# A hybrid attention and conv-FFN step on one core: five edits around two stage borders and the placement of the feed-forward operands

## The reference

```python
h = rms_norm(x, norm_attn)
qa, ka, va, qb, kb, vb = project_heads(h, ...)       # one projection, QK-norm, rope on the b part
oa = band_attn_a(qa, ka, va, rel_table)              # own chunk of 64 and 8 before it, bias by distance
ob = window_attn_b(qb, kb, vb, sinks)                # own chunk and 2 before it, with sinks
x = x + concat(oa, ob) @ w_out
h2 = rms_norm(x, norm_ffn)
gate, up = split(h2 @ w_gate_up)                     # 2 x 2816 columns
y = silu(causal_conv3(gate)) * up
x = x + y @ w_down
```

## Time and profile before

| | |
|---|---|
| Median of 3 runs | 2585.76 us (2584.2 to 2586.54) |
| Profiled execution, its own time | 2588.3 us |
| Span of its instructions | 2586.5 us, mean granted clock 0.98 |
| PE busy | 2447.7 us, 95% |
| DVE, ACT, POOL busy | 67%, 45%, 39% |
| DMA | 577.88 MB, mean 223 GB/s |
| project, attend, combine, ffn begin near | 0, 476.8, 945, 1176.5 us |

### The profile page before, as it was taken

The page is one execution under the profiler, slowest core; times in us unless marked ns, Lnnn a source line. Parts: engine busy times, 40 slices in busy tenths (PEclk is TensorE's granted clock), DMA queues, the critical chain, the costliest instruction groups (busy, mean ns, idle before and its releaser), DMA issues. The chain is left out here.

```text
span 2586.5 us, 46395 instructions
## 1 busy us (share of the span) xinstructions
PE 2447.7 (95%) x15365; PEld 2338.7 (90%) x15365; DVE 1740.0 (67%) x3774; ACT 1165.4 (45%) x2658; POOL 1003.2 (39%) x1153
## 2 busy tenths in 40 slices
PE   6999999589999979997999999999999999999998
PEld 4888888489999979987899999989999998999997
DVE  7667565466767755777676666766666777666766
ACT  6232322377776753334444443543444454444433
POOL 2888888557788778841220000213000021000001
PEclk9999999789999989998999999999999999999999
DMA  8776766656666659878686666878766677666665
GB/s 257 218 225 207 222 209 193 149 143 178 177 164 182 184 168 350 299 278 310 218 295 214 210 209 214 302 235 301 221 210 216 214 265 263 209 212 213 218 202 182
DMA packets 318493, 577.88 MB, mean 223 GB/s; under 512 B 35490, under 2 KB 168082, under 8 KB 318178
## 3 DMA queue, kind: packets, MB, share of 16 engines
q1 hardware_dynamic: 274288, 423.85, 51.9%
q0 software_dynamic: 39728, 149.36, 18.1%
q10 hardware_dynamic: 4290, 2.31, 0.4%
HBM read 444.88 MB, written 132.10 MB: 223 GB/s over the span
## 5 line engine op out<-in xcount | busy, mean ns | idle before, releaser
L2170 PE MATMUL ffn_x<-carry_big 128*128 128x352 f32 x2508 | 461.9, 325 | 17.6 <-PEq L62 13.5
L2170 PEld LDWEIGHTS ffn_x<-carry_big 128*128 128x128 f32 x2508 | 414.4, 189 | 22.6 <-issue 20.4
L2170 PE MATMUL ffn_z<-ffn_h_hi_S,carry_big 128*128 128x352 f32 x1056 | 283.7, 330 | 17.3 <-DVE carry_big L2311 11.2
L316 PE MATMUL project_z<-project_w_hi,project_h_hi 128*128 128x512 f32 (+3 forms) x680 | 256.3, 377 | 20.1 <-DVE project_w_lo L489 16.0
L316 PE MATMUL project_z<-project_w_lo,project_h_hi 128*128 128x512 f32 (+3 forms) x680 | 252.5, 371 | 0.0
L316 PE MATMUL project_z<-project_w_hi,project_h_lo 128*128 128x512 f32 (+3 forms) x680 | 252.4, 371 | 0.0
L2071 POOL TENSOR_TENSOR carry_x<-carry_x,carry_work 128x352 f32<-128x352 f32 x48 | 52.2, 1088 | 514.2 <-DVE carry_work L2429 455.8
L2065 POOL DMA_DIRECT2D carry_work<-h_sums_scratch x8 | 4.4, 552 | 584.0 <-DVE ffn_y_lo_S L2333 579.6
L2311 DVE TENSOR_TENSOR carry_big<-carry_w_raw,carry_big 128x512 fp32r<-128x512 f32 (+2 forms) x413 | 225.2, 553 | 0.7 <-ACT carry_big L2250 0.4
L946 PE MATMUL attend_o<-attend_v,attend_prob_t 128*128 (+1 forms) x1680 | 213.1, 271 | 0.0
L946 PEld LDWEIGHTS attend_o<-attend_v,attend_prob_t 128*128 128x128 f32 x1680 | 211.0, 194 | 0.6
(11 more groups left out here) (259 smaller groups left out, 6534.5 us busy)
## 6 DMA issues: line engine op xcount, KB each, us to landing
carry_big<-t_gu_scratch SPq DMA_DIRECT2D x264, 512.0 KB, 4.0
carry_big<-t_dn_scratch SPq DMA_DIRECT2D x240, 256.0 KB, 3.3
carry_w_raw<-w_gu SPq DMA_DIRECT2D x198, 256.0 KB, 4.1
t_gu_scratch<-project_quads POOLq DMA_DIRECT2D x68, 512.0 KB, 4.5
carry_w_raw<-w_dn SPq DMA_DIRECT2D x180, 128.0 KB, 3.5
project_quads<-w_quads POOLq DMA_DIRECT2D x68, 256.0 KB, 4.6
carry_w_raw<-w_o SPq DMA_DIRECT2D x24, 512.0 KB, 6.0
t_dn_scratch<-attend_quads POOLq DMA_DIRECT2D x22, 512.0 KB, 4.4
```

Of the source, the lines that this page charges most:

```text
L316: last = nc.tensor.matmul(z[c][0:w, 0:width], h[:, k, 0:w], ww[:, k, first:first + width], start=(k == 0 and h is hi and ww is w_hi), stop ...
L2170: mm = nc.tensor.matmul(bank[:, 0:SUB], weights(c)[:, wp, k, :], (hi, lo)[a][name][:, 1 if short else k, :], start=first and k == 0 and (w ...
```

## The change

1. **attend.** The cache loads go to SP ahead of everything, and the first tile's queries go from SP to ACT behind bias, far and sink. The identity and the cached values go to POOL, ahead of its memsets. The caches' lo parts go from POOL to DVE, behind the bias and ahead of `split_first`.
2. **combine, sums.** S3, S1, S2 are made by DVE in step 2, s = 0, of the last block, S4 in step 3, s = 0. S3's split moves from step 3, s = 0, to step 2, s = 1. POOL keeps the two loads and the two stores. A12 gets a buffer of its own and is loaded by SP in step 2, behind the next weights and ahead of the stores of x1 and h2. S4 takes the buffer of A11.
3. **Last square.** The square of the last row tile moves from combine to ffn's c0 on ACT (`last_square`), and its addition to DVE at c0 (`last_add`). DVE adds the one before it inside the last step.
4. **Norm in ffn.** PE's sum moves from c0 to c5, ACT's root from c0 to c6, DVE's correction from c0 to c7 and the eight `last_norm` from c4..c11 to c8..c15. ACT's wait for A12's lo part at c3 is gone.
5. **Placement.** `gate` is allocated before the operands and not behind them.

```diff
# attend
@block.sync
-            load(0)
+            for (first, count, cache), src in zip(caches, (ka_cache..., kb_cache...)):
+                twice(cache, src, cache_ld)
+            twice(raw[:, HEADS:HEADS + KV_A, 0:DEC], k_a[:, :, SEQ:]..., ld)
+            twice(raw[:, HEADS + KV_A:, 0:DEC], qk_b[PAIRS_B:, :, SEQ:]..., ld)
+            sp.dma_start(v[0:DEC, TILES + 1, :], v_all[SEQ:, :]).then_inc(ld, 16)
             load_b(0)
@block.gpsimd
+            pool.dma_start(ident_sb[:], ident).then_inc(const_ld, 16)
+            pool.dma_start(v[:, TILES, 0:PAIRS_A * P], va_cache).then_inc(const_ld, 16)
+            pool.dma_start(v[:, TILES, PAIRS_A * P:], vb_cache).then_inc(const_ld, 16)
...
-            for i, (head, count, cache) in enumerate(caches):
-                part = keys[HEAD:, head:head + count, SEQ:SEQ + P]
-                pool.wait_ge(k0_hi, i + 1)
-                nc.gpsimd.tensor_tensor(part, cache[HEAD:, :, :], part.bitcast(F32), ALU.subtract).then_inc(k0_ok, 1)
@block.scalar
-            (cache loads, ident, va_cache, vb_cache)
+            for i in range(2):
+                nc.scalar.dma_start(raw[i * HEAD:(i + 1) * HEAD, 0:HEADS, 0:DEC], q_a[:, :, SEQ:]...).then_inc(ld, 16)
@block.vector
             dve.wait_ge(bias_set, 1)
+            for i, (head, count, cache) in enumerate(caches):
+                part = keys[HEAD:, head:head + count, SEQ:SEQ + P]
+                dve.wait_ge(k0_hi, i + 1)
+                nc.vector.tensor_tensor(part, cache[HEAD:, :, :], part.bitcast(F32), ALU.subtract).then_inc(k0_ok, 1)
             split_first()
# Carry
-        self.last_c = by_sub(part(0))
+        self.last_sq, self.last_t, self.last_r = part(1), by_sub(part(1)), by_sub(part(0))
-        self.first_raw = {"A12": self.stage[0], ...}
+        self.first_raw = {"A12": self.p_sum, ...}
# combine, SP
                     load_w(g + 1)
+                if (b, i) == (LAST, 2):
+                    sp.wait_ge(c_ok, LAST)
+                    stored(sp, range(HALF_K, KD))
+                    sp.dma_start(kept.first_raw["A12"], h2T[HALF_K:KD, :, 0:SUB]...).then_inc(kept.h0_ld["A12"], 16)
...
             pass_on(LAST, PAIRS - 1)
-            sp.wait_ge(kept.h_lo_ok, HALF_K)
-            sp.wait_ge(sums_ok, 3)
-            stored(sp, range(HALF_K, KD))
-            sp.dma_start(kept.first_raw["A12"], ...)
# combine, ACT
-                    square(b, 2 * i + s)
+                    if (b, i, s) != (LAST, PAIRS - 1, 1):
+                        square(b, 2 * i + s)
...
+                    if (b, i, s) == (LAST, 2, 1):
+                        split_first("S3")
                     if (b, i, s) == (LAST, PAIRS - 1, 0):
-                        split_first("S3")
                         split_first("S2")
# combine, DVE
+                    if (b, i, s) == (LAST, PAIRS - 1, 1):
+                        add_square(LAST, KD - 2)
                     add(b, i, s, 0)
...
+                    if (b, i, s) == (LAST, 2, 0):
+                        sum_s3()
+                        sums_s1_s2()
+                    if (b, i, s) == (LAST, 2, 1):
+                        split_first("S3")
                     if (b, i, s) == (LAST, PAIRS - 1, 0):
-                        split_first("S3")
+                        sum_s4()
                         split_first("S2")
...
-            for s in range(2):
-                add_square(LAST, KD - 2 + s)
# combine, POOL
-                (waits and the four tensor_tensor of L1671 to L1679)
                 pool.wait_ge(sums_ok, 2)
+                pool.dma_start(h_sums[0, 0], lower[1]).then_inc(sums_st[0], 16)
                 pool.wait_ge(sums_ok, 4)
+                pool.dma_start(h_sums[0, 3], kept.stage[0]).then_inc(sums_st[1], 16)
# ffn
+    LAST_NORM = 6
+        gate = m.sbuf("gate", [P, H + BLOCK])
         h_hi, h_lo = ...
         y_hi, y_lo = ...
-        gate = m.sbuf("gate", [P, H + BLOCK])
-            pool.wait_ge(last_c, 1)
+            pool.wait_ge(h_lo_ok, h_done(0, "A12", HK - 1))
             pool.dma_start(first_raw["S4"], h_sums[0, 3]).then_inc(h0_ld["S4"], 16)
-                if c == 0:                       # PE
+                if c == LAST_NORM - 1:
+                    pe.wait_ge(last_sum, 1)
                     (the sum of squares into kept.ms)
-                if c == 3:                       # ACT
-                    act.wait_ge(h_lo_ok, h_done(0, "A12", HK - 1))
-                if c == 0:
+                if c == LAST_NORM:
                     last_root()
                 if c == 0:                       # DVE
-                    last_scale()
+                    last_add()
+                if c == LAST_NORM + 1:
+                    last_scale()
-                if 4 <= c < 4 + KD:
-                    last_norm(c - 4)
+                if LAST_NORM + 1 < c <= LAST_NORM + 1 + KD:
+                    last_norm(c - LAST_NORM - 2)
```

More of the change, by code:

```diff
@@ L790, in store @@
                     .then_inc(o_st[mixer], 16)
-            load(0)
+            for (first, count, cache), src in zip(caches, (ka_cache.rearrange(by_heads, p=HEAD), kb_cache.rearrange("(a p) n -> p a n", p=HEAD))):
+                twice(cache, src, cache_ld)
+            twice(raw[:, HEADS:HEADS + KV_A, 0:DEC], k_a[:, :, SEQ:].rearrange(by_heads, p=HEAD), ld)
+            twice(raw[:, HEADS + KV_A:, 0:DEC], qk_b[PAIRS_B:, :, SEQ:].rearrange(by_heads, p=HEAD), ld)
+            sp.dma_start(v[0:DEC, TILES + 1, :], v_all[SEQ:, :]).then_inc(ld, 16)
             load_b(0)
@@ L1070, in _ @@
             nc.scalar.dma_start(sink[:], sinks.rearrange("(a n) -> a n", a=1)).then_inc(sink_ld, 16)
-            for (first, count, cache), src in zip(caches, (ka_cache.rearrange("f (a p) n -> p (f a) n", p=HEAD),
-                                                           kb_cache.rearrange("(a p) n -> p a n", p=HEAD))):
-                for i in range(2):
-                    nc.scalar.dma_start(cache[i * HEAD:(i + 1) * HEAD], src).then_inc(cache_ld, 16)
-            nc.scalar.dma_start(ident_sb[:], ident).then_inc(const_ld, 16)
-            nc.scalar.dma_start(v[:, TILES, 0:PAIRS_A * P], va_cache).then_inc(const_ld, 16)
-            nc.scalar.dma_start(v[:, TILES, PAIRS_A * P:], vb_cache).then_inc(const_ld, 16)
+            for i in range(2):
+                nc.scalar.dma_start(raw[i * HEAD:(i + 1) * HEAD, 0:HEADS, 0:DEC], q_a[:, :, SEQ:].rearrange("f (a p) n -> p (f a) n", p=HEAD)).then_inc(ld, 16)
             act.wait_ge(cache_ld, 64)
@@ L1252, in __init__ @@
         self.carry, self.tail, self.state = (self.small[:, i * 2 * KF:(i + 1) * 2 * KF].rearrange("p (f n) -> p f n", n=2) for i in range(3))
-        self.first_raw = {"A12": self.stage[0], "S1": self.s_all, "A22": self.y_raw, "S4": self.p_sum}
+        self.first_raw = {"A12": self.p_sum, "S1": self.s_all, "A22": self.y_raw, "S4": self.p_sum}
         flat = lambda first, count: self.big[:, first:first + count]
@@ L1402, in _ @@
                     load_w(g + 1)
+                if (b, i) == (LAST, 2):
+                    sp.wait_ge(c_ok, LAST)
+                    stored(sp, range(HALF_K, KD))
+                    sp.dma_start(kept.first_raw["A12"], h2T[HALF_K:KD, :, 0:SUB].rearrange("k p n -> p k n")).then_inc(kept.h0_ld["A12"], 16)
                 if b < LAST:
@@ L1421, in _ @@
             pass_on(LAST, PAIRS - 1)
-            sp.wait_ge(kept.h_lo_ok, HALF_K)
-            sp.wait_ge(sums_ok, 3)
-            stored(sp, range(HALF_K, KD))
-            sp.dma_start(kept.first_raw["A12"], h2T[HALF_K:KD, :, 0:SUB].rearrange("k p n -> p k n")).then_inc(kept.h0_ld["A12"], 16)
             sp.wait_ge(z_ok[0][1], PAIRS * N_BLOCKS)
@@ L1617, in split_first, with sum_s3, sums_s1_s2, sum_s4 @@
                                             kept.operand[name, 0][:, k, :].bitcast(F32), ALU.subtract).then_inc(kept.h_lo_ok, 1)
+            a11 = s4 = kept.stage[0]
+            a21, a22 = lower
+            def sum_s3():
+                dve.wait_ge(first_ld, 16)
+                dve.wait_ge(sums_ld[0], 16)
+                nc.vector.tensor_tensor(kept.stage[1], a11, a21, ALU.subtract).then_inc(sums_ok, 1)
+            def sums_s1_s2():
+                dve.wait_ge(sums_ld[1], 16)
+                nc.vector.tensor_tensor(a22, a21, a22, ALU.add).then_inc(sums_ok, 1)
+                dve.wait_ge(sums_ok, 2)
+                nc.vector.tensor_tensor(a21, a22, a11, ALU.subtract).then_inc(sums_ok, 1)
+                dve.wait_ge(sums_ok, 3)
+            def sum_s4():
+                dve.wait_ge(kept.h0_ld["A12"], 16)
+                nc.vector.tensor_tensor(s4, kept.first_raw["A12"], a21, ALU.subtract).then_inc(sums_ok, 1)
             nc.vector.memset(eps[:], EPS).then_inc(eps_ok, 1)
@@ L1904, in ffn @@
         h0_ld = kept.h0_ld
-        last_ms, last_ln, last_r, last_r2, last_t, last_c, last_h2, last_st = (
-            m.sem(n) for n in ("last_ms", "last_ln", "last_r", "last_r2", "last_t", "last_c", "last_h2", "last_st"))
```

(10 more changed lines are left out.)

23 lines of the change are left out of this document (7 added, 16 removed).

## The result

The changed kernel takes 2567.65 us (median; 2562.31 to 2568.84, 4 runs), the kernel before 2584.98 beside it. The ratio is 0.9929, with a 95% interval of 0.9911 to 0.9946: 17.3 us less (20.4 between the profiled executions). The forecast was 24.3 less.

What follows compares the result with a forecast made beforehand. PE, busy 95% of the span, was taken as the bound. Terms 2.5 + 13.1 - 0.3 + 9 = 24.3 us took the median from 2585.8 to 2561.5; own range 2556 to 2567 (chance 0.70), full range 2552 to 2572.

Steps and rivals of the forecast that it cites:

- DVE becomes the bound in step 2: Rival, combine's last block: slow sums or stores holding L1609 make PE stall; 6 us more, 2567.5; chance 0.09.
- Attend, 2.5 us: Start of attend: new load order and lo parts on DVE end it at 493.9 or 494.2, not 496.73; gain 2.5 us.
- attend gains nothing: Rival, start of attend: loads from three queues land later, so no gain there; 2564 us; chance 0.05.
- DVE is free of bias work at 489.58: Step for attend's start: DVE finishes bias at 492.78 - 3.20 and can then make the caches' lo parts.
- Combine, last step, 6.4 us: Before combine's last step: PE's 3.5 us stall and 2.9 us at half clock go, with 1.3 us of slack.
- Border, 6.7 us: Between combine and ffn: earlier sums and store let ffn start sooner; 6.7 us more, 13.1 together with combine's last step.
- with the same 7.2 us to PE's start: Border step: the last store goes at 1156.8 and PE starts 7.2 us later, as before, at 1164.0.
- A border ended by SP's or POOL's landings at the old distance: Sign that the forecast is wrong, at the border between combine and ffn; the forecast expected a PE gap of about 7 us.
- The other chain: Border: DVE's remaining work ends at 1160.8, then two short issues on SP and the barrier, about 1163.
- Start of ffn, loss of 0.3 us: First products of ffn: 0.7 + 1.1 gained, 1.2 + 1.2 lost, some of c8's weight wait gone; ends +2 and -3.
- Placement, 9 us: ffn's products with operands of their own: 0.02 us less per 12 matmuls, as in `carry_big`; gain 9 us, ends 0 and 13.
- placement gives nothing: Rival, ffn's products: PE's difference comes from something else that `carry_big` has; 2570.5 us; chance 0.13.

Runs made afterwards that it cites:

- attend_undone: The changed kernel with attend's loads and the caches' lo parts put back as in the kernel before: 2564.11 us, ratio 0.9923.
- s2_short: The changed kernel with S2's lo part made for 16 of 352 columns in combine's last step: 2566.69 us, ratio 0.9925.
- norm_soon: The changed kernel with LAST_NORM = 1: PE's sum follows c0, ACT's root c1, norms c3 to c10: 2568.35 us, ratio 0.9948.
- norm_plan: The changed kernel with PE's sum, ACT's root and DVE's scaling back in c0, norms in c4 to c11, last square still in ffn: 2560.07 us.

## Why the prediction was right, and where it wasn't

The sign held, and so did the range of 2552 to 2572. But 2567.65 lies outside the forecast's own range of 2556 to 2567 by 0.65, and near the sum of a rival, *DVE becomes the bound in step 2*, which did not happen. Three terms came short and the placement gave more than its price; that the one partly made up for the others is luck. Step by step:

- **Attend, 2.5 us: 0 to 0.4.** The rival *attend gains nothing* held, with the reason it gave (loads from three queues land later), though the load is the sinks' and not kb. The step that failed is "DVE is free of bias work at 489.58": it took the sinks' landing from the trace of before, and with the new order they are there later (DVE is free at 490.10, with a first issue that is 2.0 earlier, so 2.5 us later counted from that issue). What the Trainium skill (Trainium Kernel Development and Optimization, Key Constraints) says of shared DMA engines was cited for this very part, and the runs agree with it: with three issuing queues and not two the first scores came 0 to 0.4 us sooner.
- **Combine, last step, 6.4 us: 6.4.** 37.2 to 30.8. The stall and the half clock behind it went together; DVE's durations (1.62, 0.9, 0.45) were as worked out. The slack was not: it is 0.56 us and not 1.3, since a store of h2 holds the second of step 2's three norms for 1.07 us, which the rival *DVE becomes the bound in step 2* had as one of its conditions ("stores hold L1609"). The forecast had "Nothing else is behind it". In attend_undone that wait is 2.48 us, PE stalls 0.75 us and the last step takes 1.0 us more; so the term came in whole by a slack that other executions use up.
- **Border, 6.7 us: 3.4.** The step that failed is "with the same 7.2 us to PE's start": they hold the landing of a store that had little traffic beside it, and they are 9.5 now (6.0 of landing and not 3.6). The store also goes out 0.55 us after PE's last matmul and not 0.1. "A border ended by SP's or POOL's landings at the old distance" stood among the signs of being wrong; POOL's landing does end it, at a longer distance. The other chain was mis-sized as well ("then two short issues on SP and the barrier: about 1163", where 3.4 us alone lie between the last landing and the first instruction of ffn), but s2_short shows that it isn't the last.
- **Start of ffn, loss of 0.3 us: 4 to 5 by the norm's new place, and up to 3.4 of chance.** The sum had PE's own 1.2 and c9's 1.2, both of which came (1.2 and 1.4); it costed nothing for the weights, which c27 and c28 now wait for, and named only the accumulator's load as late next. norm_soon and norm_plan show that the norms' place makes that wait. The accumulator's load is issued 48.9 us after ffn's start, and was 37.4 after it: 11.6 us later, not 8. That the waits come through the norms' stores and these loads was argued and not tried alone.
- **Placement, 9 us: 12 to 13 by the medians, 15 to 17 at equal clock, 18 to 20 by the traces.** The mechanism was right and the size off: 0.02 us for a product was the difference to `carry_big`'s products, which were taken for the clean pace. They were held back too: it is 0.05 us for the others (1.96 to 1.91) and 0.02 for them. The rival *placement gives nothing* fell, and with it, for this kernel, what the Trainium skill (SBUF — State Buffer, Specifications) would give: both starts meet its 16 bytes, and 2.5 ns of 162 lie between them.

The terms that came short (attend 2.3, border 3.3, ffn's start 5 or more) add up to 10.6 us or more. The placement gave 3 to 11 us more than its 9, by the measure that one takes; with 3.5 the sum is about the 17.3 measured.

## What to carry to other kernels

When a step is moved earlier, price the transfers that wait at a stage's end with the traffic they will then meet: a landing time read where little else runs does not move along. Before taking a reorder for free, list what else keeps its distance from it: here eight norms moved by four products also moved their stores and the loads behind them by 11 us, and weights 12 products on came late. A matmul's moving operand should be tried at another start in SBUF when products that differ only in that show different paces, and the fast kind is not proof of the clean pace.

## What was not expected of the hardware

- The start of the moving operand in SBUF changes the pace of fp32r matmuls of 352 columns from 163.1 to 159.3 ns (96 bytes off a multiple of 128, and on it; 160.2 at 64 off). It also changes the matmuls of other products between them whose operands did not move (161.4 to 159.1).
- After nearly the same idle time (9.8 to 10.2 us) and with the same instructions, ffn's fourth product started 9.0 to 9.2 us after the first in two executions and 12.6 us in three, as the granted clock went from 0.50 to 1.00 by the second product or only about the start of the fourth.
- A store of 704 KB landed after 3.6 to 4.8 us with little beside it, and after 5.5 to 6.2 us beside other stores and a load of weights. The row of 8 sinks was there 9.5 us after its issue behind bias and far, and 1.2 us after it when first.
- From the landing that POOL waits for at combine's end to the first instruction of DVE in ffn it took 3.40 us in all fourteen traces.
